# A slab's 640 token columns cut into 512 and 128 instead of 320 and 320, in layer 1's input projection of a diffusion trunk

## The reference, cut to what matters

```python
h = _rmsnorm(x, W["norms"][l, 1]) * (1 + sc2) + sh2
...
q, k, v = jnp.split(h @ W["w_in_c"][j], 3, axis=-1)      # (tokens, 1024) @ (1024, 3072)
```

## Time and profile before

| what | value |
|---|---|
| time, median of 3 runs | 4068.52 us (4064.79 to 4070.91) |
| profiled execution, span | 4070.0 us; the profile states no time of its own beside it |
| mean granted clock of TensorE | 0.874 |
| TensorE busy | 3540.9 us, 22346 matmuls |
| VectorE busy | 1839.3 us |
| ScalarE busy | 998.3 us |
| slab matmuls of the stage | 1152, from 2917.5 to 3089.3 us |

### The profile page before, as it was taken

The page is one execution under the profiler, slowest core; times in us unless marked ns, Lnnn a source line. Parts: engine busy times, 40 slices in busy tenths (PEclk is TensorE's granted clock), DMA queues, the critical chain, the costliest instruction groups (busy, mean ns, idle before and its releaser), DMA issues.

```text
span 4070.0 us, 55614 instructions
## 1 busy us (share of the span) xinstructions
PE 3540.9 (87%) x22346; PEld 3286.8 (81%) x22346; DVE 1839.3 (45%) x2902; ACT 998.3 (25%) x1729; POOL 0.2 (0%) x4
## 2 busy tenths in 40 slices
PE   7899998875979797978999989999897555799998
PEld 7899998854868686868999989999895222699997
DVE  2554545443454544445545455554413555332223
ACT  1212122232121212122121232112323444232212
POOL 0000000000000000000000000000000000000000
PEclk6899999965877776879999999999998666899999
DMA  6344441100000000022444424343220000122221
GB/s 193 89 119 119 119 115 56 29 0 19 1 4 1 4 1 2 1 58 60 121 114 114 124 83 117 106 127 110 78 72 7 5 5 25 52 64 81 72 73 57
DMA packets 393639, 264.46 MB, mean 65 GB/s; under 512 B 11627, under 2 KB 375430, under 8 KB 393222
## 3 DMA queue, kind: packets, MB, share of 16 engines
q1 hardware_dynamic: 393478, 262.23, 22.8%
HBM read 258.13 MB, written 4.06 MB: 64 GB/s over the span
## 4 chain that ended last, share of the span: by engine, by line
PE 83%; DVE 10%; ACT 3%; issue 3%; DMA 1%; SPq 0%; DVEq 0%; ACTq 0%
PE pair L1960 56%; PE pair L761 5%; PE pair L1946 2%; PE pair L1274 1%; PE pair L1969 1%; PE pair L1926 1%; DVE big L1780 1%; PE pair L721 1%; PE pair L799 1%; PE pair L722 1%; PE pair L756 1%; PE pair L802 1%; PE pair L1269 1%; DVE w_lo_as_f L1383 1%; PE pair L421 1%
## 5 line engine op out<-in xcount | busy, mean ns | idle before, releaser
L1960 PE MATMUL pair<-h_hi,w_hi 128*128 128x320 f32 x3792 | 875.7, 312 | 120.3 <-DVE h_lo L1789 68.1
L1960 PE MATMUL pair<-h_lo,w_hi 128*128 128x320 f32 x3792 | 873.1, 312 | 0.0
L1960 PE MATMUL pair<-h_hi,w_lo 128*128 128x320 f32 x3792 | 872.3, 312 | 0.0
L1960 PEld LDWEIGHTS pair<-h_hi,w_hi 128*128 128x128 f32 x3792 | 642.1, 190 | 124.1 <-issue 124.1
L1960 PEld LDWEIGHTS pair<-h_lo,w_hi 128*128 128x128 f32 x3792 | 642.8, 190 | 0.0
L1960 PEld LDWEIGHTS pair<-h_hi,w_lo 128*128 128x128 f32 x3792 | 641.7, 190 | 0.0
L1960 PE MATMUL pair<-big_as_f32r,w_hi 128*128 128x320 f32 x2816 | 538.8, 314 | 4.6 <-DVE w_lo L1679 4.4
L1569 ACT ACTIVATE w_hi<-raw 128x1024 fp32r<-128x1024 f32 x333 | 341.3, 1052 | 630.9 <-PE pair L1960 333.0
L1679 DVE TENSOR_TENSOR w_lo<-raw,w_hi 128x1024 fp32r<-128x1024 f32 x333 | 397.5, 1216 | 163.5 <-ACT w_hi L1569 162.7
L1960 PEld LDWEIGHTS pair<-big_as_f32r,w_hi 128*128 128x128 f32 x2816 | 451.3, 192 | 5.6 <-DVE w_lo L1679 5.2
L1824 DVE TENSOR_TENSOR work<-work,pair 128x640 f32<-128x640 f32 x88 | 72.2, 821 | 644.0 <-PE pair L1960 644.0
(11 more groups left out here) (345 smaller groups left out, 3571.1 us busy)
## 6 DMA issues: line engine op xcount, KB each, us to landing
raw<-ffn_w SPq DMA_DIRECT2D x272, 512.0 KB, 5.0
work<-mod_w SPq DMA_DIRECT2D x136, 512.0 KB, 3.8
raw<-w_in_c SPq DMA_DIRECT2D x24, 512.0 KB, 3.8
raw<-w_in_ab SPq DMA_DIRECT2D x21, 512.0 KB, 3.9
w_hi_as_f<-mod_w SPq DMA_DIRECT2D x8, 512.0 KB, 4.7
raw<-w_out_ab SPq DMA_DIRECT2D x8, 512.0 KB, 5.4
raw<-w_out_c SPq DMA_DIRECT2D x8, 512.0 KB, 5.1
h_hi_as_f<-x_sample SPq DMA_DIRECT2D x1, 2048.0 KB
```

Source lines behind the costliest of these rows:

```text
L1960: ins = nc.tensor.matmul(ps[:, c, 0:HALF], w, v[:, k, c * HALF:(c + 1) * HALF], start=(k == 0 and w is hi and v is xh), stop=(k == kts - 1 ...
```

## The change

In layer 1's input projection alone, the two matmuls of each product take token columns 0 to 512 and 512 to 640, into bank 0 and the first 128 columns of bank 1. The 640 sums of a slab then lie next to each other in PSUM, and ScalarE evicts them with one contiguous read of 640 columns instead of two pieces of 320. All other stages keep 320 and 320.

```diff
-                        nc.scalar.activation(halves(big[:, j, :]), pp[(n0 + j) % 4][:, :, 0:HALF], ACT.Copy).then_inc(pair_free, 1)
+                        nc.scalar.activation(big[:, j, :], pp[(n0 + j) % 4][:, :, :].rearrange("p a n -> p (a n)")[:, 0:TOK], ACT.Copy
+                                             ).then_inc(pair_free, 1)
...
-            def slab(i, j, kts, k0, xh, xl, wait_tile, sections=()):
+            def slab(i, j, kts, k0, xh, xl, wait_tile, sections=(), cuts=((0, 0, HALF), (1, HALF, TOK))):
...
-                        for c in range(2):
-                            ins = nc.tensor.matmul(ps[:, c, 0:HALF], w, v[:, k, c * HALF:(c + 1) * HALF],
+                        for c, a, b in cuts:
+                            ins = nc.tensor.matmul(ps[:, c, 0:b - a], w, v[:, k, a:b],
                                                    start=(k == 0 and w is hi and v is xh),
                                                    stop=(k == kts - 1 and w is lo))
...
+                cuts = ((0, 0, LAT), (1, LAT, TOK)) if (kind, l) == ("in", 1) else ((0, 0, HALF), (1, HALF, TOK))
...
-                            slab(i2, n0 + j, kts, k0, xh, xl, tile_ready if j == 0 else None)
+                            slab(i2, n0 + j, kts, k0, xh, xl, tile_ready if j == 0 else None, cuts=cuts)
```

## The result

The changed kernel takes 4097.1 us (median of 3 runs, 4085.65 to 4100.21) against 4068.52: a ratio of 1.0057, 95% interval 1.0032 to 1.0082. The profiled execution spans 4095.2 us against 4070.0.

A forecast was written before the change was run, and what follows sets the result against it. TensorE's matmul pace was taken to bound the kernel. A pair at 215 + 147 = 362 ns against 293, 69 ns more times 576, gave 39.5 us on the median of 4068.5: 4108 us, range 4085 to 4160.

The forecast's parts named there:

- The stage is TensorE's: Layer 1's input projection: TensorE's pace sets the stage, busy in all 165.50 us of the undisturbed part; 576 pairs at 293.3 ns.
- The eviction costs nothing: ScalarE's 24 evictions of 705 ns: one piece adds 0 to 0.04 us each, nothing on the path.
- The mechanism: Likeliest case, layer 1's input projection: a floor under the 128-column piece, between 110 and 147 ns; chance 0.48.
- The plain price: Rival: the 128-column piece costs 222 ns as in the plain two-instruction form; pair 437 to 449 ns, 4151 to 4158; chance 0.34.
- only columns count: Rival: 13.3 ns paid per matmul, loads hidden behind either piece; pair 294 ns, time stays 4068.5; chance 0.10.
- faster: Rival: long piece hides the load's remainder and short loads are quick; pair 271 ns, 4056; chance 0.04.
- the clock: Rival: short pieces make TensorE's granted clock fall from 1.00 to 0.50; 427 + 147 ns a pair, 4230; chance 0.04.
- the 13.3 ns: Time each 320-column matmul of the stage takes beyond its columns' 133.3 ns; read as explained by a floor, not a charge.
- the 147 ns: Pace of the stage's 320-column matmuls, the one this form had shown, taken as the 128-column piece's price.
- wrong if the short piece comes out well away from 147 ns: The prediction's own sign of failure for the 128-column piece; time moving outside the stage was the other.
- the likeliest case: A floor under the 128-column piece, between 110 and 147 ns; point 4108, own range 4087 to 4115; chance 0.48.
- the low-clock row, with nothing over: Stage's first 5 us at clock 0.50: 267 ns per 320-column matmul, no surplus; held to speak against a charge per matmul.

## Why the prediction was right, point by point

**The stage is TensorE's** and every nanosecond of a pair is paid 576 times: right. The stage grew by 27.25 us and nothing else by a like amount.

**The eviction costs nothing**: right, by the changed kernel (706 ns, off the path) and by the run with two reads.

**The mechanism**, a floor under the short piece that the long one can't make good: right. Short pieces follow each other at 0.11 us, and half the columns save nothing. The floor goes by the width of the weights, as the run with 64 columns shows, though not whether by the load or by the partitions written. The plain price was excluded by the 340 ns a pair and by 192 instructions of each width; "only columns count" and "faster" by the time itself; the clock by 1.00 in the stage.

**The sizes** were off in two terms, in opposite directions. The failed step is the reading of the 13.3 ns: "I take 215, as the surplus is explained by a floor that a piece so long lies above". The surplus is a charge on the matmuls of this form at the high clock. It stayed with narrow weights, with pieces of 512 columns (226.7 ns) and without bank changes; where it comes from isn't shown. So the long piece is 227 ns, the other bound in the text. And the 147 ns of 320 columns were never a floor, so the short piece isn't 147 but 340 - 227 = 113 ns, next to the 109 to 112 ns of the plain short matmuls. Long 12 ns too cheap, short 34 too dear: 22 ns a pair, 12.7 us of the 39.5. What was left, with 0.4 us from the low clock, is the stage's 27.25 us. By its own sign ("wrong if the short piece comes out well away from 147 ns") the prediction had the short piece's size wrong. That the point came within 11 us is in part luck: with the long piece alone put right the sum would have been 46 us, with the short piece alone 20. The time still lies in the likeliest case's own range of 4087 to 4115, which has both right values near its bounds: 227 + 110 ns give 25 us.

**The argument against a charge per matmul** ("the low-clock row, with nothing over") was a wrong inference: at 1.2 GHz 320 and 512 columns show no surplus, at 2.4 GHz both show 13.3 ns. A charge at one clock only was taken for no charge.

The Trainium skill ("TensorE: Matmul & The Clock Gate", section on LDWEIGHTS) gave 107 ns for such a load, and the short piece came out at 113; the estimate made with it, 17 us, fell short by 12 ns a pair in the long piece and 6 in the short one. At the low clock the runs show 213 ns for the same short piece, so the floor is no fixed time: it nearly doubles where TensorE's clock halves.

No cut of all 640 columns tried here beats the kernel before: 384 and 256 gives the same time, since both pieces lie above the floor, and with 448 and 192 or 512 and 128 the floor adds 20 and 47 ns a pair.

## What to carry to other kernels

Where every matmul brings its own weights, price a cut as the sum of max(columns and a fixed charge, floor of the weight load) over the pieces: an uneven cut is free until its short piece meets the floor, and then its missing columns are paid as if they were there. With 13.3 and 113 ns this gives the pairs of every cut here with weights of 128 columns within 3 ns, at a granted clock of 1.00; other forms and widths of weights have to be measured. Of two readings of a surplus in the only shape that a trace shows, a charge per instruction or a floor, neither can be chosen from that shape; carry both through the sum. Measure unlike matmuls by their period, not from start to start.

## What was not expected of the hardware

A stage of 1152 rounded matmuls of 128 columns, TensorE without a gap, kept the clock at 0.50 for all of its 246 us: 256 columns a pair, two fifths of the changed kernel's 640, took longer (10.24 us a slab) than all of them (8.16). In the other runs, with pairs of 512 and 64 columns too, the clock rose from 0.50 to 1.00 during the stage's first slab. Plain matmuls of 64 and 128 columns, 109 to 112 ns apart, had kept 1.00 in layer 0's mixer. TensorE being busy in the profile is thus no sign that the full clock is granted; what decides isn't shown here, and the stage of short pieces was run once.
